# Order of loads and stores, and the unit-by-unit split of expert weights, in a fused encoder layer on one core

## The reference, cut to what matters

```python
h = rmsnorm(x, g_mix); proj = h @ w_in                       # q, k, v, z, xbc, dt, two gates
ya = windowed_gqa(q, k, v, sink, bias) @ w_attn_out
ys = ssd_branch(z, xbc, dtf, dtb, ...) @ w_ssd_out           # conv, scans both ways, gated norm
x = x + (sigmoid(ga) * ya + sigmoid(gs) * ys) @ w_out
h = rmsnorm(x, g_ffn)
# each token: one of 4 groups, the best 2 of its 4 experts; 16 experts, w_gate_up 1024 x 512, w_down 256 x 1024
x = x + sum_e gates[e] * ((silu(g_e) * u_e) @ w_down[e])     # g_e, u_e = split(h @ w_gate_up[e])
x = x + sigmoid(rmsnorm(x, g_ple) @ w_ple_gate) * (p @ w_ple_proj)
y = rmsnorm(x, g_final)
```

## Time and profile before

| | |
|---|---|
| runs | 1906.66, 1909.68, 1919.39 us; median 1909.68 |
| profiled execution | 1917.14 us, its span 1915.3 us |
| granted PE clock, mean | 0.955 |
| PE busy | 1755.6 us, 92% of the span |
| DVE, ACT, POOL busy | 888.0, 602.4, 424.3 us |
| DMA | 265.91 MB, mean 139 GB/s |
| scan begins / experts' first block / output stage's first product | 909.0 / 1387.6 / 1777.5 us |

### The profile page before, as it was taken

One profiled execution on the slowest core, in us unless ns is written; L12 is line 12 of the kernel. 1 busy time (PEld: TensorE's weight loads), 2 busy tenths in 40 slices (PEclk: granted clock), 3 DMA queues, 4 the chain that ended last, 5 costly groups with the idle time before them and its releaser, 6 DMA issues. The chain is left out here.

```text
span 1915.3 us, 27128 instructions
## 1 busy us (share of the span) xinstructions
PE 1755.6 (92%) x10464; PEld 1435.9 (75%) x10465; DVE 888.0 (46%) x1024; ACT 602.4 (31%) x1007; POOL 424.3 (22%) x282
## 2 busy tenths in 40 slices
PE   6998999889999979988999998998899997996897
PEld 5876888777877847777788886786677876784685
DVE  5201776202133137731688422522668786901774
ACT  4201222230111126632355212312534442442432
POOL 3001111111211110002100021200156655652430
PEclk8999999999999989989899999999899998998898
DMA  5212222323355221016566242322757776733553
GB/s 195 82 34 68 85 74 81 110 62 108 124 182 181 88 77 40 26 66 210 169 189 167 103 145 102 124 79 81 281 187 268 258 292 215 295 112 130 189 176 99
DMA packets 115837, 265.91 MB, mean 139 GB/s; under 512 B 13011, under 2 KB 59555, under 8 KB 115740
## 3 DMA queue, kind: packets, MB, share of 16 engines
q1 hardware_dynamic: 99484, 209.11, 32.8%
q0 software_dynamic: 8320, 30.43, 4.7%
q10 hardware_dynamic: 7936, 25.01, 3.7%
HBM read 192.95 MB, written 71.55 MB: 138 GB/s over the span
## 5 line engine op out<-in xcount | busy, mean ns | idle before, releaser
L2030 DVE TENSOR_TENSOR ex_wlo<-ex_raw,ex_whi 128x1024 fp32r<-128x1024 f32 x96 | 150.3, 1579 | 6.1 <-ACT ex_whi L2024 6.1
L275 PE MATMUL rest_p<-hi_h,whi_in 128*128 128x512 f32 (+1 forms) x480 | 123.5, 366 | 12.1 <-POOL wlo_in L894 6.7
L2587 PE MATMUL rt_p<-ex_whi,ex_xh 128*128 x280 | 115.3, 412 | 14.2 <-issue 7.8
L2026 DVE CAST ex_whi<-ex_raw 128x1024 fp32r<-128x1024 f32 x90 | 93.6, 1046 | 70.2 <-DMA ex_raw<-experts 68.9
L275 PE MATMUL rest_p<-lo_h,whi_in 128*128 128x512 f32 (+1 forms) x480 | 121.2, 361 | 0.0
L275 PE MATMUL rest_p<-hi_h,wlo_in 128*128 128x512 f32 (+1 forms) x480 | 120.6, 360 | 0.0
L2589 PE MATMUL rt_p<-ex_whi,ex_xl 128*128 x280 | 111.2, 397 | 0.0
L2588 PE MATMUL rt_p<-ex_wlo,ex_xh 128*128 x280 | 111.2, 397 | 0.0
L275 PEld LDWEIGHTS rest_p<-hi_h,whi_in 128*128 128x128 f32 x480 | 81.1, 191 | 34.5 <-POOL wlo_in L894 7.6
L865 ACT ACTIVATE rest_out<-rest_p 128x1024 f32<-128x1024 f32 x20 | 20.5, 1026 | 257.5 <-PE rest_p L275 257.5
L894 POOL TENSOR_TENSOR wlo_in<-wraw_in,whi_in 128x1024 fp32r<-128x1024 f32 x18 | 43.7, 2432 | 222.6 <-ACT whi_in L859 222.6
(11 more groups left out here) (382 smaller groups left out, 4089.9 us busy)
## 6 DMA issues: line engine op xcount, KB each, us to landing
ex_raw<-experts SPq DMA_DIRECT2D x96, 512.0 KB, 6.2
wraw_in<-units SPq DMA_DIRECT2D x36, 512.0 KB, 3.7
y_slots<-ex_y ACTq DMA_DIRECT2D x35, 512.0 KB, 3.5
rest<-rest_out SPq DMA_DIRECT2D x20, 640.0 KB, 6.1
scan_e<-erow SPq DMA_DIRECT2D x32, 256.0 KB, 4.4
xtok<-conv_tok SPq DMA_DIRECT2D x10, 640.0 KB, 3.3
z_x<-x SPq DMA_DIRECT2D x10, 512.0 KB, 4.0
ao_gate<-rest SPq DMA_DIRECT2D x8, 640.0 KB, 5.8
```

The source lines that it names most:

```text
L275: mm = pe.matmul(out[:, n, 0:size], w[:, kk, :], h[:, kk, c:c + size], start=(kk == 0 and w is whi and h is hi), stop=(kk == ktiles - 1 an ...
L2026: eng.tensor_copy(self.hi[:, e % 2, n, :], self.raw[e % 2][:, n, :]).then_inc(self.w_hi[n], 1)
L2030: eng.tensor_tensor(self.lo[:, e % 2, n, :], self.raw[e % 2][:, n, :], self.hi[:, e % 2, n, :].bitcast(F32), ALU.subtract).then_inc(self.w ...
L2587: pe.matmul(gu[s][:, :], xh[s][:, kk, :], hi, start=(kk == 0), stop=False)
```

## The change

Four places, some of them hanging together:

1. Out-attention: SP loads the gate of c + 2 before it stores product c, and calls `early` after the store of c = 5, no longer before that of c = 4.
2. Route: only expert 0's six loads stand ahead of the stores of p; expert 1's follow one by one behind the stores of tiles 0 to 5.
3. Experts: DVE casts a unit, subtracts it, and waits for its own subtraction before the next. The ring is used once more, as for an expert 16, for gate units 0 to 5.
4. Output: the gate's units 0 to 5 lie in the ring, 6 and 7 are loaded and split by ACT and DVE (class `GateUnits`); the tiles' buffers have other places; tile 2's gather stands before the root of tile 1; the last tile's p is loaded into tile 0's place once that is free.

```diff
@@ stage_out_att, sync
-            if c == 4:
-                early(sp)
             sp.wait_ge(used, c + 1)
-            sp.dma_start(d["mix_a"][c * P:(c + 1) * P, :], prod[c % 2][:, :]).then_inc(stored[c % 2], 16)
             if c + 2 < KT:
                 load_gate(c + 2)
+            sp.dma_start(d["mix_a"][c * P:(c + 1) * P, :], prod[c % 2][:, :]).then_inc(stored[c % 2], 16)
+            if c == 5:
+                early(sp)
@@ ExpertWeights.load
-        sp.dma_start(self.raw[e % 2][:, n, :], self.k.d["experts"][at:at + P, :]).then_inc(self.w_in[e % 2][n], 16)
+        w = self.k.d["experts"][at:at + P, :] if e < N_EXP else self.k.d["units"][U_PG + n]
+        sp.dma_start(self.raw[e % 2][:, n, :], w).then_inc(self.w_in[e % 2][n], 16)
@@ stage_route, sync
-            for e in range(2):
-                for n in range(6):
-                    ew.load(sp, e, n)
+            for n in range(6):
+                ew.load(sp, 0, n)
             for t in range(NT):
                 sp.wait_ge(pp_copied, t + 1)
                 sp.dma_start(d["pp"][t * P:(t + 1) * P, :], out[t % 2][:, :]).then_inc(pp_stored[t % 2], 16)
+                if t < 6:
+                    ew.load(sp, 1, t)
@@ stage_experts, sync
-            for e in range(2, N_EXP):
+            for e in range(2, N_EXP + 1):
@@ stage_experts, vector
-            for e in range(1, N_EXP):
-                ew.split_hi(dve, e, 0)
+            for e in range(1, N_EXP + 1):
                 for n in range(6):
-                    if e == 1 and n == 3:
+                    if e == 1 and n == 4:
 
                         for s in range(2):
                             dve.wait_ge(pp_stored[s], 16 * (NT // 2))
-                    if n < 5:
-                        ew.split_hi(dve, e, n + 1)
+                    ew.split_hi(dve, e, n)
                     ew.split_lo(dve, e, n)
+
+                    dve.wait_ge(w_lo[n], e + 1)
@@ new
+class GateUnits:
...
+        self.lo = [ew.lo[:, 0, n, :] for n in range(6)] + [k.at(f"pg_lo{n}", [P, 1024], F32R, O_W + n * 4096) for n in (6, 7)]
+        self.hi = [ew.hi[:, 0, n, :] for n in range(6)] + [k.at(f"pg_hi{n}", [P, 1024], F32R, O_W + (n + 2) * 4096) for n in (6, 7)]
...
+    def wait_unit(self, pe, n):
+        if n >= 6:
+            pe.wait_ge(self.w_lo, n - 5)
@@ stage_output
-        w = ResidentUnits(k, "pg", U_PG, [O_ST + 4096 * j for j in range(4)])
+        w = GateUnits(k, ew)
...
-                sp.dma_start(second[:, t, :], d["pp"][t * P:(t + 1) * P, :]).then_inc(p_in[t % 2], 16)
+                if t < NT - 1:
+                    sp.dma_start(second[t][:, :], d["pp"][t * P:(t + 1) * P, :]).then_inc(p_in[t % 2], 16)
                 if t:
                     store(t - 1)
+                if t == 2:
+
+                    sp.wait_ge(gated, 1)
+                    sp.dma_start(second[0][:, :], d["pp"][(NT - 1) * P:NT * P, :]).then_inc(p_in[2], 16)
...
             norm.root(pool, 0)
+            gather(2)
             norm.root(pool, 1)
-            w.split_lo(pool, 1)
-            w.split_lo(pool, 3)
-            gather(2)
-            w.split_lo(pool, 5)
-            w.split_lo(pool, 7)
...
             square(1)
+            for n in (6, 7):
+                w.split_hi(act, n)
             split(0)
-            for n in range(8):
-                w.split_hi(act, n)
...
             norm.apply(dve, 1, x[:, 1, :], xn[1][:, :])
+            w.split_lo(dve, 6)
             rest(0)
-            for n in range(0, 8, 2):
-                w.split_lo(dve, n)
+            w.split_lo(dve, 7)
```

More of the change, by code:

```diff
@@ L2708, in store @@
                 sp.wait_ge(final.normed, t + 1)
-                sp.dma_start(out, first[:, t, :]).then_inc(stored, 16)
+                sp.dma_start(out, first[t][:, :]).then_inc(stored, 16)
             norm.load(sp)
@@ L2771, in split @@
                 act.wait_ge(turned, t + 1)
-                act.activation(hi[:, t, :, :], tp[t % 2][:, :, :], ACT.Copy).then_inc(hi_s, 1)
+                act.activation(hi[t][:, :, :], tp[t % 2][:, :, :], ACT.Copy).then_inc(hi_s, 1)
             square(0)
             square(1)
+            for n in (6, 7):
+                w.split_hi(act, n)
             split(0)
-            for n in range(8):
-                w.split_hi(act, n)
             for t in range(NT + 1):
@@ L2783, in _ @@
                     act.wait_ge(tile_done, t)
-                    act.activation(first[:, t - 1, :], zp[(t - 1) % 2][:, :], ACT.Sigmoid).then_inc(sig, 1)
+                    act.activation(first[t - 1][:, :], zp[(t - 1) % 2][:, :], ACT.Sigmoid).then_inc(sig, 1)
                 if t + 2 < NT:
@@ L2788, in _ @@
                     act.wait_ge(added, t)
-                    final.square(act, t - 1, x[:, t - 1, :], first[:, t - 1, :])
+                    final.square(act, t - 1, x[:, t - 1, :], first[t - 1][:, :])
         @block.tensor
@@ L2822, in combine @@
                     xt = x[:, t, :]
-                    dve.scalar_tensor_tensor(out=xt, in0=view[:, t, :], scalar=r.weight[:, n, t:t + 1], in1=xt,
+                    dve.scalar_tensor_tensor(out=xt, in0=view[t][:, :], scalar=r.weight[:, n, t:t + 1], in1=xt,
                                              op0=ALU.mult, op1=ALU.add).then_inc(combined if n else part, 1)
@@ L2859, in _ @@
                     final.scale(dve, t - 1)
-                    final.apply(dve, t - 1, x[:, t - 1, :], first[:, t - 1, :])
+                    final.apply(dve, t - 1, x[:, t - 1, :], first[t - 1][:, :])
 def build(nc, dram, upto=99):
@@ L2908, in build @@
     k.clear_semaphores()
-    stage_output(k, r, x1)
+    stage_output(k, r, x1, ew)
 def _units(w_in, w_attn_out, w_ssd_out, w_out, w_ple_gate, w_ple_proj):
```

37 lines of the change are left out of this document (26 added, 11 removed).

## The result

The changed kernel takes 1884.37 us (median of four executions, 1880.81 to 1887.58) against 1910.77 us in the same session: a ratio of 0.9856, 95% interval 0.9816 to 0.9895, 26.4 us less. Timed again beside the last experiments it gave 0.9856 once more (0.9817 to 0.9894); one of the six executions of that session, at 4379 us, counts as slow and is left out. The forecast was 1876, its range 1861 to 1894.

What follows compares the result with a forecast made beforehand. PE was taken to hold the end nearly everywhere, with its standstills and low clock to be won; 7 + 6 + 9 + 11.8 = 33.8 us off the median of 1909.7 gave 1876, range 1861 to 1894.

Steps and rivals of the forecast that it cites:

- Out-attention, 7 forecast: Start of the scan: earlier gate loads start the sums 5.6 us earlier, plus 1.4 for the clock; ends 2 and 13.
- Stores of p first, 6 forecast: Route stage: PE's 4.66 us wait and 2.2 us of half clock go, later transfers take some back; ends 0 and 8.
- Experts, 9 forecast: Experts: 8.3 + 1.5 + 1.2 - 2 us from the new order and waits of DVE's splits; ends -6 and 12.
- The release of POOL: Experts: the gap after every DVE instruction lets POOL in, so PE's 8.32 us of waits for `ex_hid` go.
- 16 x 0.38 = 6 us later, of which I let PE see 2: Experts 10 to 12: two 0.19 us waits in each of 16 units delay DVE by 6 us; PE loses 2.
- 1.5 of the 4.8 us go: Expert 10: unit 0 is subtracted at once, which takes 1.5 us off PE's 4.8 us of waits for low halves.
- the third rival: Experts: DVE becomes the bound, all 34 us of waits are on the path, 9 us slower, 1919 us; chance 0.06.
- Output stage, 11.8 forecast: Output stage: product 1 of the gate starts 8.5 us earlier, the end gains 3.3; ends 5 and 13.5.
- the low end: Output stage: only 5 us gained, with tile 1's root held up on POOL by the third gather, and low clock.
- POOL shut out: Experts: the 0.11 us gap may not let POOL in; experts give -2 and not 9, 1887 us; chance 0.14.
- Only moved waits: Scan start and stores of p: early transfers only move the waits; 24.8 us gained, 1885 us; chance 0.12.
- The output stage gaining its tail alone: Output stage: tile 2's `cm_xn`, not the weights, held product 1; 5 us, not 11.8, 1883 us; chance 0.10.

Runs made afterwards that it cites:

- e11: The changed kernel run once more, unaltered; profiled span 1880.5 us against 1885.3 in its first profile.
- e5: The changed kernel with the out-attention's SP stream as before (chunk 0 ahead of gates 6 and 7, stores ahead of loads); 1892.9 us, 0.9903 of the kernel before.
- e6: The changed kernel with all 12 expert loads ahead of the stores of p again; 1891.3 us, 0.9911 of the kernel before.
- e1: The changed kernel with the experts' splits as before (next unit's cast ahead of the subtraction, no wait behind it); 1894.3 us, 0.9879 of the kernel before.
- e4: The kernel before with the changed experts' splits alone (cast, wait, subtraction, wait); 1903.6 us, 0.9954 of the kernel before.
- e7: The changed kernel with the output stage of before and no gate units in the experts' ring; 1893.4 us, 0.9908 of the kernel before.
- e8: The changed kernel with the third gather issued behind root(1) instead of ahead of it; 1884.1 us in a single execution.
- e2: The changed kernel without the wait behind each subtraction, one pause a unit left ahead of the subtraction; 1883.5 us, 0.9829 of the kernel before.
- e3: The changed kernel with the old order of the splits but the wait behind each subtraction kept; 1882.8 us, 0.9838 of the kernel before.
- e9: The changed kernel without DVE's casts for experts 9 to 13, output not the reference's; 1879.8 us in a single execution.
- e10: The changed kernel without POOL's low half of x in blocks 17 to 24, output not the reference's; 1876.6 us in a single execution.

## Why the prediction was right, and what was off

The direction, the four places and the range held; 1876 was 8.4 too low. Of that, 1.1 is the median of before (1910.77 for 1909.68), 3.8 the sum (33.8 against 30.0 in the spans), and most of the remaining 3.5 that the profiled execution of before lay further above its median (1917.1 for 1910.8) than the changed kernel's (1887.6 for 1884.4).

- *Out-attention, 7 forecast.* 9.2 in the first pair of profiles, 7.4 in e11, 7.6 to 9.4 by e5. The eleven profiles with the new order against the three with the old give 6.7; the 9.2 was a favourable pair. The sums were put at 903.4 and started at 903.18. As feared, the low clock stayed: 0.50 from 905 to 920.
- *Stores of p first, 6 forecast.* 5.2, and 4.8 to 4.9 by e6. The 4.7 us wait went. The 2.2 us of low clock behind it did too, but the changed kernel's first matmuls of p ran at 0.50, where those of before had not; that took some 2 us back. The kernels whose first matmuls ran at 1.00 are 6 to 8 us below before in that column.
- *Experts, 9 forecast.* 6.8 and 7.7. The release of POOL was right: no `ex_hid` above 1.8 us, its waits 8.6 us less against 8.3 forecast, and e1 and e4 show it both ways. The term that was mis-sized is "16 x 0.38 = 6 us later, of which I let PE see 2", together with "1.5 of the 4.8 us go". The wait costs 0.12 and not 0.19, and in the 20th block late low halves held PE for 4.4 us instead of 4.8, so the semaphores alone cost nothing that shows there. But the 23rd block got 5.3 us longer, 3.0 of it waiting, beside a cast of 2.75 us in place of 0.69: POOL's low half of x stopped DVE. Such stops were there before, too (a cast of 2.86 us at 1580.16); my sum had no term for one at a place where PE waits for DVE next. Where experts of one block follow each other DVE is the bound, as the third rival said, for that stretch only. I had named waits above 10 us as a sign of being wrong; the view has 11.5, of which 7.4 were for low halves that were late. By lengths of blocks the 20th gave 9.5 us, the two behind it 1.6, the 23rd took 5.3, the first gave 2.6, the rest of the stage took 1.6. The first block's 2.6 were no part of my sum and went with the granted clock (0.74 and 1.00): that 6.8 came so near to 9 is in part luck. Without the 23rd block's stall the stage is 9 to 12.5 us shorter than before (e4, e6, e7, e8).
- *Output stage, 11.8 forecast.* 9.6, and 10.4 to 11.9 by e7. The end gave 3.2 (13.6 to 10.4 us from the last matmul's start to the span's end) for 3.3. Product 1 came 6.2 us closer to product 0 and not 7.5, since product 0 ran 4.2 us at 0.50 and lasted 13.1; and product 0 did not start 1 us earlier (25.4 us behind the last expert matmul, before 25.5). Before, it had waited 1.82 us for `pg_lo`; now it waits 0.30 for tile 0's low half, but tile 0's turn came 0.4 us later and tile 1's, which stands between, waited 0.87 for its `cm_xn`. That is the hold-up of tile 1's root by the third gather that I had named for the low end (e8 has 0.16 and starts product 0 0.7 us sooner).
- *The rivals.* POOL shut out: excluded by e2, e3 and e4. Only moved waits: excluded by e5 and e6. The output stage gaining its tail alone: excluded by e7 and the timelines, 10.4 to 11.9 us of which the tail is 3.2. DVE the bound of the whole stage: no, but of its middle.
- *The signs.* Four came: sums at 903.18 with both gate loads out by 889.12, no wait for `pp_out`, no `ex_hid` above 1.8 us, DVE's last product right behind the last sigmoid. Three of the small ones didn't: a block of 15.4 us stayed (15 was the limit), product 1 came 13.9 us behind product 0 (under 13; 12.9 in e11), and DVE's instructions are 0.03 to 0.04 apart and not 0.1.

The rule of the Trainium skill ("SBUF — State Buffer", section "Who interferes with whom") was set against the trace; as I worked it out, POOL would wait for one DVE instruction. It fails again in e1: POOL's 0.74 us of work took 10.70 us, across more than ten DVE instructions. For DVE with pauses it fits: the longest `ex_hid` are 1.6 to 1.8 us. And it fits 46 of the 47 starts beside splits without a pause in before, and 44 of the 45 in e1, with at most 1.1 us lost, less than one subtraction of 1.21.

## What to carry to other kernels

A row of DVE instructions, each starting before the last has ended, can keep POOL out until the row ends (once in each of the two traces without pauses); with one wait of 0.12 us for an own semaphore every second instruction that didn't occur in any of twelve traces. But what POOL gains, DVE pays, so before freeing POOL add POOL's time to DVE's and compare the sum with PE's, stretch by stretch and not over the stage. Before counting a wait that the view names, check when the named instruction had ended: of 11.5 us "for low halves" 4.1 were none. And with terms of 5 us in a program whose executions scatter by 10, cut the profiles at fixed instructions, and use more than one pair: e6's span was 4 us below that of the kernel with the edit, while its own column was 4.8 us longer and its median 6.9 higher.

## What the runs showed that I had not expected

- One pause of 0.03 us, in place of an overlap of 0.08, went with POOL being let in every time. It doesn't matter whether it stands ahead of the cast or ahead of the subtraction.
- The same wait of PE (6.85 to 6.9 us for `rt_both`, then 0.7 to 1.3) was followed by matmuls of p 0.23 us apart in five profiles (before, e5, e8, e9, e10; granted clock 1.00), and by the first of them 0.43 apart in eight (the changed kernel, e11, e1, e2, e3, e4, e6, e7; 0.50), with the same instructions ahead of it. The difference is some 2 us, as much as the terms that are weighed here.
- A stall of 4.3 us in one block (14.7 against 10.4 us) appears or not by how DVE and POOL happen to fall, and came again, at 14.6 us, when the same kernel was run once more.
